# Decay rows of a state space layer: spread over the partitions by transfers instead of by products

## The reference, cut to what matters

```python
a_cs = jnp.cumsum(dtr * a_neg, axis=2)                 # (chunk, token, head)
decay = jnp.exp(jnp.where(causal, a_t[..., :, None] - a_t[..., None, :], -jnp.inf))
mix = cb[:, :, :, None] * decay                        # cb = C B^T of the chunk
y_diag = jnp.einsum('bcgrij,bcjgrp->bcigrp', mix, xdt)
y_off = jnp.einsum('bclgn,bcgrpn,bclgr->bclgrp', cr, h_in, jnp.exp(a_cs))
```

## Time and profile before

| | |
|---|---|
| runs | 986.08, 986.47, 987.04 us, median 986.47 |
| profiled execution | 986.6 us, span 984.5 us |
| busy, share of the span | TensorE 99%, its weight loads 97%, VectorE 62%, ScalarE 45%, GpSimd 32% |
| granted TensorE clock, mean | 0.998 |
| HBM | 116.42 MB read, 7.93 MB written |

### The profile page before, as it was taken

How to read it: one execution, slowest core, us unless ns; L and a number is a source line. 1 busy time by engine, 2 the same in 40 slices (tenths; PEclk the granted TensorE clock), 3 DMA queues, 4 the chain that set the end, 5 groups by cost and what they waited for, 6 DMA issues and landing times.

```text
span 984.5 us, 19172 instructions
## 1 busy us (share of the span) xinstructions
PE 975.0 (99%) x7866; PEld 957.3 (97%) x7866; DVE 610.4 (62%) x956; ACT 439.8 (45%) x621; POOL 310.2 (32%) x261
## 2 busy tenths in 40 slices
PE   8999999999999999999999999999999999999997
PEld 8999999999989999899999999999999999999997
DVE  6999799854555777897644356555630036666356
ACT  7744689565736774553233344343211223222120
POOL 0111111111111114524444335444334354444351
PEclk9999999999999999999999999999999999999999
DMA  8988779568666778143452222322222342221222
GB/s 272 263 188 188 154 142 165 118 140 185 142 142 137 181 156 265 44 150 109 167 188 77 87 86 87 90 92 90 67 78 81 102 129 86 85 69 53 81 62 91
DMA packets 52750, 125.25 MB, mean 127 GB/s; under 512 B 16080, under 2 KB 19024, under 8 KB 52688
## 3 DMA queue, kind: packets, MB, share of 16 engines
q1 hardware_dynamic: 43904, 97.10, 31.9%
q0 software_dynamic: 8640, 27.27, 15.7%
q10 hardware_dynamic: 144, 0.00, 0.0%
HBM read 116.42 MB, written 7.93 MB: 126 GB/s over the span
## 4 chain that ended last, share of the span: by engine, by line
PE 98%; DMA 1%; DVE 0%; SPq 0%; ACT 0%; issue 0%; DVEq 0%
PE accs L422 90%; PE accs L1451 2%; PE misc L1227 1%; PE misc L1192 1%; PE misc L1051 1%; PE misc L1232 1%; DMA xbc<-in_x 1%; PE misc L1211 0%; PE misc L1177 0%; PE misc L1377 0%; PE misc L1139 0%; PE misc L1244 0%; PE misc L1352 0%; DVE xbc L2269 0%; PE misc L1067 0%; PE misc L1201 0%
## 5 line engine op out<-in xcount | busy, mean ns | idle before, releaser
L422 PE MATMUL accs<-h_split,w_split 128*128 128x272 f32 x4608 | 584.0, 288 | 0.0
L422 PEld LDWEIGHTS accs<-h_split,w_split 128*128 128x128 f32 x4608 | 577.2, 188 | 4.9 <-issue 3.8
L422 PE MATMUL accs<-branch,w_split 128*128 128x272 f32 x2472 | 317.0, 289 | 1.9 <-DVE w_split L1491 1.2
L422 PEld LDWEIGHTS accs<-branch,w_split 128*128 128x128 f32 x2472 | 312.1, 188 | 4.8 <-DVE w_split L1491 1.7
L361 POOL TENSOR_TENSOR w_split<-w_raw,w_split 128x1024 fp32r<-128x1024 f32 (+2 forms) x104 | 233.7, 2254 | 206.1 <-ACT w_split L356 185.8
L356 ACT ACTIVATE w_split<-w_raw 128x1024 fp32r<-128x1024 f32 (+3 forms) x166 | 158.0, 960 | 198.4 <-PE accs L422 197.8
L1536 DVE SCALAR_TENSOR_TENSOR ca<-part,params,ca 128x512 f32<-128x512 f32 x120 | 82.4, 749 | 0.1
L369 POOL DMA_DIRECT2D w_split<-in_w_in_main x24 | 21.0, 876 | 145.1 <-ACT w_split L356 145.1
L2235 DVE TENSOR_TENSOR xbc<-accs,xbc 128x544 f32<-128x544 f32 x14 | 10.1, 725 | 87.6 <-PE accs L422 87.6
L355 ACT ACTIVATE w_split<-w_raw 128x1024 fp32r<-128x1024 f32 (+1 forms) x60 | 56.2, 938 | 13.1 <-PE accs L422 12.4
L2212 DVE TENSOR_TENSOR temps<-temps,mixed 128x512 f32<-128x512 f32 x22 | 40.7, 1848 | 26.5 <-ACT temps L1025 26.5
(11 more groups left out here) (283 smaller groups left out, 794.4 us busy)
## 6 DMA issues: line engine op xcount, KB each, us to landing
w_raw<-in_ffn_w_up SPq DMA_DIRECT2D x44, 512.0 KB, 3.5
w_raw<-in_w_in_main SPq DMA_DIRECT2D x28, 512.0 KB, 4.8
w_split<-in_w_in_main POOLq DMA_DIRECT2D x24, 512.0 KB, 7.9
w_raw<-in_w_gate SPq DMA_DIRECT2D x24, 512.0 KB, 3.9
w_split<-in_w_gate POOLq DMA_DIRECT2D x16, 512.0 KB, 7.9
w_raw<-in_ffn_w_down SPq DMA_DIRECT2D x16, 384.0 KB, 3.0
w_raw<-in_ffn_w_down SPq DMA_DIRECT2D x16, 320.0 KB, 2.8
xbc<-in_x SPq DMA_DIRECT2D x16, 272.0 KB, 5.7
```

Source lines behind the costliest of these rows:

```text
L422: mm = pe.matmul(accs[:, a, half, 0:HALF], w_split[:, s, wp, k * P:(k + 1) * P], rhs(s, k, xp, half), start=(first and k == 0 and n == 0), ...
```

## The change

The 16 rows are no longer split and spread by TensorE. In G2, ScalarE copies them from PSUM to 16 partitions of a spare buffer (`a_rows`), and GpSimd stores them to a scratch in HBM (`row_store`, 32 KB). In G0, GpSimd issues for each head a transfer that reads that head's row of 2 KB 128 times, once into each partition of its `c_dec` slot. `SPREAD_AFTER` gives the slot behind whose accumulating load a pair's two transfers are issued: 4 for pairs 0 and 1, then 7, 8, 10, 11, 12 and 14. In front of them GpSimd waits until the `c_dec` slots are free and until all earlier row transfers have landed. VectorE takes the differences from `c_dec`, and ScalarE takes the exponential in place. The high and low parts stay for the 32 other tokens.

```diff
@@ -37,6 +37,7 @@
 EPS = 1e-6
 EPS_SET, WARM_ZERO, ROWS_ZERO, ZEROS_A, ZEROS_X, ZEROS_F = range(1, 7)
 SLOTS = 4
+SPREAD_AFTER = {4: (0, 1), 7: (2,), 8: (3,), 10: (4,), 11: (5,), 12: (6,), 14: (7,)}
 WARM = (12, 2, 3, 8)
 
 STATE_ORDER = (4, 5, 6, 7, 0, 1, 2, 3)
@@ -242,6 +243,8 @@
             return T(2 + h % 4, SEQ)
 
         dt_rows = T(5)
+        a_rows = temps[0:HEADS, 5, 0:SEQ]
+        row_store = nc.dram_tensor("row_store", [HEADS, SEQ], F32, kind="Internal").ap()
 
         def norm_block(j):
 
@@ -646,9 +649,32 @@
             added(("A", 1), ("VU", 0))
             pool.wait_ge(acc_free[1], 4)
             pool.memset(temps[:, 0:2, 0:SKW - 1], 0.0).then_inc(sem("cleared"), 1)
-            added(("VU", 1), *(("X", i) for i in range(3)), *(("G2", i) for i in range(4)))
-
-            added(*(("G0", i) for i in range(4)), ("Z", 0))
+            added(("VU", 1), *(("X", i) for i in range(3)), ("G2", 0))
+            for s in range(SLOTS):
+                add_raw(pool, ph["G2"], 1, s)
+                if s == 2:
+                    pool.wait_ge(sem("a_hi"), 1)
+                    pool.dma_start(row_store, a_rows).then_inc(sem("a_spread"), 16)
+            added(("G2", 2), ("G2", 3))
+
+
+            def spread(pair):
+
+                if pair < 2:
+                    pool.wait_ge(sem("cbm"), 2)
+                else:
+                    pool.wait_ge(sem("y_head"), 2 * pair - 2)
+                pool.wait_ge(sem("a_spread"), 16 + 32 * pair)
+                for h in (2 * pair, 2 * pair + 1):
+                    pool.dma_start(c_dec[h % 4], row_store[h].partition_broadcast(P)).then_inc(sem("a_spread"), 16)
+
+            added(("G0", 0))
+            for name, i in (*(("G0", i) for i in range(1, 4)), ("Z", 0)):
+                for s in range(SLOTS):
+                    add_raw(pool, ph[name], i, s)
+                    k_now = 4 * (i if name == "G0" else 4) + s - SLOTS
+                    for pair in SPREAD_AFTER.get(k_now, ()):
+                        spread(pair)
 
             pool.wait_ge(sem("y_head"), HEADS)
             pool.memset(c_masked.rearrange("p g b i -> p (g b i)"), 0.0).then_inc(sem("c_masked"), 1)
@@ -883,10 +909,11 @@
                         .then_inc(sem("dec_exp"), 1)
                 if (i, s) == (0, 2):
                     act.wait_ge(sem("a_turned"), 1)
-                    act.activation(a_split[0:HEADS, 0:SEQ], misc[0:HEADS, 2], ACT.Copy)
+                    act.activation(a_rows[:, :], misc[0:HEADS, 2], ACT.Copy)
                     act.activation(a_split[0:HEADS, SEQ:TOK], misc[0:HEADS, 3, 256:256 + SMP], ACT.Copy)\
                         .then_inc(sem("a_hi"), 1)
                 if (i, s) == (1, 2):
+                    act.wait_ge(sem("a_spread"), 16)
                     squares(ca, "cf")
                 if (i, s) == (2, 0):
                     sqrt_table()
@@ -925,7 +952,7 @@
                     act.wait_ge(sem("diff"), h + 1)
                     if h >= 4:
                         act.wait_ge(sem("y_head"), h - 3)
-                    act.activation(c_dec[h % 4], misc[:, h % 2], ACT.Exp).then_inc(sem("a_exp"), 1)
+                    act.activation(c_dec[h % 4], c_dec[h % 4], ACT.Exp).then_inc(sem("a_exp"), 1)
                 for h in groups[4 * i + s]:
                     act.activation(head_decay(h), head_decay(h), ACT.Exp).then_inc(sem("pair_decay"), 1)
             ev = evac_branch("G0", 0, 0)
@@ -1202,15 +1229,6 @@
                                        start=True, stop=True)
                     mm.then_inc(sem("cb"), 1)
 
-            def spread(h):
-
-                if h == 0:
-                    pe.wait_ge(sem("cbm"), 2)
-                if h >= 2:
-                    pe.wait_ge(sem("a_exp"), h - 1)
-                pe.matmul(misc[:, h % 2], head_of[:, h:h + 1].to_broadcast([P, P]), a_split[:, 0:SEQ],
-                          start=True, stop=True).then_inc(sem("a_spread"), 1)
-
             def y_pair(h0):
 
                 b0, pair = 2 + (h0 // 2) % 2, (h0, h0 + 1)
@@ -1305,8 +1323,6 @@
                     for h in heads[k - 2] if k >= 2 else ():
                         if h % 2 == 0:
                             y_pair(h)
-                    for h in heads[k]:
-                        spread(h)
                 return between
             p = ph["G0"]
             rhs = merge_rhs(conf_at)
@@ -1749,8 +1765,6 @@
             def split_rows():
 
                 dve.wait_ge(sem("a_hi"), 1)
-                dve.tensor_tensor(a_split[32:48, 0:SEQ], misc[0:HEADS, 2], a_split[0:HEADS, 0:SEQ].bitcast(F32),
-                                  ALU.subtract)
                 dve.tensor_tensor(a_split[32:48, SEQ:TOK], misc[0:HEADS, 3, 256:256 + SMP],
                                   a_split[0:HEADS, SEQ:TOK].bitcast(F32),
                                   ALU.subtract).then_inc(sem("a_rows"), 1)
@@ -1918,12 +1932,12 @@
 
             def diffs(h):
 
-                dve.wait_ge(sem("a_spread"), h + 1)
+                dve.wait_ge(sem("a_spread"), 16 + 32 * (h // 2 + 1))
                 if h >= 4:
                     dve.wait_ge(sem("y_head"), h - 3)
                 for c in range(NCH):
                     cols = slice(c * CH, (c + 1) * CH)
-                    ins_ = dve.tensor_scalar(head_decay(h)[:, cols], misc[:, h % 2, cols],
+                    ins_ = dve.tensor_scalar(head_decay(h)[:, cols], c_dec[h % 4][:, cols],
                                              small[:, A_CUM, c * HEADS + h:c * HEADS + h + 1], 0.0,
                                              ALU.subtract, ALU.min)
                 ins_.then_inc(sem("diff"), 1)
```

## The result

The changed kernel takes 1014.6 us (median of 6 runs, 1013.6 to 1015.3), the kernel before 986.3 us on the same chip: a ratio of 1.0286, 95% interval 1.0275 to 1.0296. The profiled execution has a span of 1012.1 us against 984.5, so 27.6 us are to be explained.

A forecast was written before the change was run, and what follows sets the result against it. TensorE, 98% of the chain that ended last, was taken to bound the kernel. Spreads -3.7, gaps +23.1 and clock +6 sum to +25.4 us on the profiled 986.6 us: 1012 us, range 992 to 1030 (chance 0.80).

The forecast's parts named there:

- The spreads: TensorE in G0: sixteen spreading products go, two for each of eight pairs, -3.7 us, at most 4.5.
- A pair lands 9.6 us after its slot's load is issued: G0, GpSimd's queue: rows start when the 512 KB load ahead is through, 7.9 us, plus 1.7 for the pair.
- The sign that the prediction named: G0: row transfers land about 8 to 9 us after their issue in slots with a 512 KB load ahead.
- The gaps: TensorE in G0 waits 4.3 us for pair 0, 2.0 each for 3 and 6, 7.4 each for 4 and 7: 23.1.
- A pair's chain: G0, from a pair's first difference to its last scaled C row: stays at 5.94 us, within half a microsecond.
- The clock: TensorE behind the gaps of 4.3, 7.4 and 7.4 us: lowered clock costs 2 us each, 6 us in all.
- The sum: Whole kernel: -3.7 + 23.1 + 6 = +25.4 us, giving 1012 us.
- Hidden transfers: Rival for G0: all gaps vanish and 3.7 us are won, 982.8 us; chance 0.04.
- Quick landing: Rival for G0: nothing queues, rows land 2.6 us after issue, +0.5 us, 987.0 us; chance 0.05.
- Slow rows: Rival for G0: 128 reads of one 2 KB row are slower than of 128 rows, about 1021 us; past 1030, chance 0.11.
- Weights behind GpSimd's waits: G0: accumulating loads held behind GpSimd's waits for rows still meet their slots, cost nothing, 6 us in hand.
- the store: G2: GpSimd's store of the rows, one issue of 0.87 us, and ScalarE's wait for it cost nothing.

The follow-up runs named there:

- kernel without rows: Changed kernel without the row transfers and VectorE's waits for them, first exponential with scale 0, store of the rows kept: 982.8 us, 0.9968 of the kernel before.
- kernel that was kept busy: Changed kernel plus unread TensorE products in the gaps before slot 7 and the head products of pairs 4 and 7: 1011.9 us, 1.0266 of the kernel before.
- six rows: Changed kernel with row transfers issued in front of the weight loads, two more row buffers and issues a pair earlier: 982.6 us, 0.9964 of the kernel before.
- other rows: Changed kernel, but each partition reads its own 2 KB of a weight tensor instead of all reading one row: 1012.5 us, 1.0261 of the kernel before.
- rows first: Changed kernel, each pair's transfers but pair 1's issued before the accumulating load they followed, after the previous slot's load: 987.2 us, 1.0011 of the kernel before.
- order only: Changed kernel, each place's first pair issued immediately before its accumulating load, at the same moment within 0.6 us: 1004.0 us, 1.0175 of the kernel before.

## Why the prediction was right, point by point

The forecast was 1012 us, the kernel takes 1014.6, and the mechanism is the forecast one in outline: rows that arrive late, issued behind a weight load, with TensorE standing in front of a few slots and head products, and the clock falling behind the long gaps. Inside it, the path of the rows was forecast too simply, and some of the terms fit partly by luck.

- *The spreads*, -3.7 us: 3.5 net by the kernel without rows. Right.
- *A pair lands 9.6 us after its slot's load is issued.* From the load's issue to the first difference it is 9.4 us for pair 4 (349.17 to 358.56), 9.3 for pair 7 and 8.4 for pair 0. The size is nearly right, the reading behind it only in part. The place in the queue does count: swapping the order gave back 10.6 us. But the rows don't start when the load ahead of them is through. Pair 4's first transfer, issued at 349.77, took 6.6 us and so landed at 356.4, 0.8 us before the load ahead of it (349.17 and 8.0 us: 357.2); pair 7's did the same. The transfers run beside each other, and it was partly luck that 7.9 + 1.7 came to the measured 9.4. Issue to landing of that one transfer:

```profile
ca<-row_store POOLq DMA_DIRECT2D x1, 256.0 KB, 6.6
```

Nor did show a load on its own: 5.2 us before the 256 KB load at 254.62, GpSimd had issued one of 512 KB at 249.39, which was in flight until 256.8 (kernel before: timeline, then time to landing):

```profile
249.39 0.88 POOL L369 DMA_DIRECT2D w_split<-in_w_gate  x1 [5.86 <-ACT w_split L356]
...
w_split<-in_w_gate POOLq DMA_DIRECT2D x1, 512.0 KB, 7.4
```

That fits what the experiments show: 5.2 us in front of the load, 7.3 to 7.4 right behind it, 6.0 to 9.7 on another queue near the start of a load, 3.3 to 4.7 late in its flight or with none. The sign that the prediction named, 8 to 9 us from a pair's own issue behind a 512 KB load, was too high: pairs 0, 4 and 7 took 6.8 to 7.4.

- *The gaps*, 23.1 us: 26.1. Forecast and measured: slot 7 4.3 and 3.04, slot 11 2.0 and 1.12, pair 4 7.4 and 9.57, slot 15 2.0 and 1.00, pair 7 7.4 and 9.45, pair 2 nothing and 1.91. The short ones were too large. For slot 7 that is pair 0, which landed 1.2 us sooner behind its load than forecast. Slots 11 and 15 came by another path: the rows of pairs 3 and 6 did not go out right behind their slot's load but 4.7 and 2.5 us behind its issue, when GpSimd's wait for the landing of pairs 2 and 5 ended (first two lines below), and then took 4.4 and 4.3 us. Pair 2 was forecast to cost nothing, but with only 256 KB of weights ahead its rows took 8.3 us, the slowest landing of this kernel (third line; issued at 326.06 and 326.62). SyncE's store and load of the states (325.49 and 325.99) were in flight then; whether they slowed the rows no run isolates.

```profile
336.04 1.16 POOL L669 DMA_DIRECT2D u_sb<-row_store  x2 [3.81 <-DMA ca<-row_store]
371.80 1.16 POOL L669 DMA_DIRECT2D ca<-row_store  x2 [1.59 <-DMA u_sb<-row_store]
...
ca<-row_store POOLq DMA_DIRECT2D x2, 256.0 KB, 8.3
```

The two long ones were too small because I took today's issue time of the load. It moves: pair 3's late exponentials stand on ScalarE in front of the emptying and split of slot 10, so load 10 goes out 5.0 us later behind its slot, while the moment at which pair 4 is due moved by only 2.8. That is 7.4 + 5.0 - 2.8 - 0.2 (9.4 instead of 9.6) + 0.1 (the chain) = 9.5. For pair 7 the load goes out 2.8 us later behind its slot and the due moment moves by 0.7: 7.4 + 2.8 - 0.7 - 0.3 + 0.1 = 9.3. Late work delayed the issue of the next rows; I read this from the timeline, and no run isolates it.

- *A pair's chain*, 5.94 us: from pair 4's first difference to its last scaled C row it is 5.37 (358.56 to 363.93), because a difference from SBUF takes less, not more; but the head products also wait for `y_sum` (L1956), which stands behind the scaling, and so 6.08 us in all.
- *The clock*, 6 us: 5.4 by the rows (1.6 in slot 7, 1.5 and 1.5 in the head products, 0.8 in slot 16), of which the kernel that was kept busy confirms 3.8. Right, though it named the gaps of 4.3 and more and didn't know where the price starts.
- *The sum.* -3.7 + 26.1 + 5.4 = +27.8, measured +27.6. The gaps came out 3.0 us larger and the clock 0.6 smaller than forecast: that is nearly all of the 2.6 us by which the forecast was low.
- *The rivals.* Hidden transfers: what it would give, 982.8 us, is what the kernel without rows and the one with six rows take; so its price was right and its condition, an earlier issue, was not met by this change. Quick landing, for which the fit of the Trainium skill's "DMA: Bandwidth & Descriptors" ("Anatomy of one DMA") spoke with an estimated 2.6 us: no pair's two transfers took less than 3.2 us on the mean in any run, and in the changed kernel none less than 3.8. Slow rows: other rows took the same time to within 2 to 2.5 us.
- *Weights behind GpSimd's waits* and *the store*, nothing each: no wait of TensorE for a transfer appears in G0, in any of these kernels. Right.

## What to carry to other kernels

A transfer that replaces a little work of the bounding engine is paid for in lateness: write down when its buffer comes free, what has to happen before it can be issued, and how long it lands beside the loads that run then, and compare that with the moment at which its reader is due. If it is late, issue it earlier or give it another buffer, before looking for a faster queue: here the same sixteen transfers cost 28 us behind the weight loads, 1 us in front of them, and won 3.6 us with two more buffers and an issue one pair earlier. And look at which engine's order carries the lateness on: a late operand in front of the instruction that releases the next load makes the next operand later still.

## What the runs showed of the hardware

- A transfer that ScalarE issues did not wait for the activations in front of it: issued at 344.61 us, while the split that stands before it in the program ran at 347.97.
- Rows of 2 KB read 128 times from one place in HBM landed as fast as 128 different rows: medians of 6.9 and 5.5 us against 6.7 and 5.4.
- The same rows of 256 KB took 3.3 to 9.7 us to land (mean of a pair's two), depending on what else was in flight and how long it had been.
- A transfer issued 0.6 us behind an accumulating load of 512 KB on the same queue landed 0.8 us before it (pair 4: 356.4 against 357.2).
- The differences take 286 ns from SBUF and 342 ns from PSUM, while an exponential of a row takes 631 ns from SBUF and 596 from PSUM. The group of the differences from the changed kernel, and from the kernel before (busy us, mean ns):

```profile
L1940 DVE TENSOR_SCALAR temps<-ca,small 128x128 f32<-128x128 f32 x32 | 6.7, 286 | 27.9 <-DMA ca<-row_store 27.9
```

```profile
L1926 DVE TENSOR_SCALAR temps<-misc,small 128x128 f32<-128x128 f32 x64 | 17.3, 342 | 8.6 <-PE misc L1211 8.5
```

- TensorE's gaps of 1.91 us (the changed kernel) and 1.99 us (rows first) cost no clock, one of 2.10 us (order only) and those of 2.68 us and more did. In the changed kernel the lowered clock cost 1.5 to 2.3 us behind each of its three gaps of 3.04 us and more.
